# Two accumulating DMAs in another order on GpSimd's queue

## The reference, cut to what matters

```python
def swiglu_ffn(h, w_gu, w_down):
    g, u = jnp.split(h @ w_gu, 2, axis=-1)
    return (jax.nn.silu(g) * u) @ w_down       # mid: 512 x 2816, w_down: 2816 x 1024
...
x = x + 0.5 * swiglu_ffn(rmsnorm(x, n_ffn2[i]), ffn2_w_gu[i], ffn2_w_down[i])
```

## Time and profile before

| what | value |
|---|---|
| median of 3 runs | 1913.32 us (1913.1 to 1913.39) |
| the profiled execution | 1913.59 us |
| its span, first to last instruction | 1911.9 us |
| TensorE busy in it | 1901.3 us (99%) |
| VectorE, ScalarE, GpSimd busy | 1433.0, 1017.2, 361.8 us |
| mean granted TensorE clock | 0.999 of full speed |
| chain that ended last, by engine | PE 96%, DVE 2%, ACT 1%, issue 1% |

### The profile page before, as it was taken

The page is one execution under the profiler, slowest core; times in us unless marked ns, Lnnn a source line. Parts: engine busy times, 40 slices in busy tenths (PEclk is TensorE's granted clock), DMA queues, the critical chain, the costliest instruction groups (busy, mean ns, idle before and its releaser), DMA issues.

```text
span 1911.9 us, 33151 instructions
## 1 busy us (share of the span) xinstructions
PE 1901.3 (99%) x12350; PEld 1740.7 (91%) x12350; DVE 1433.0 (75%) x2272; ACT 1017.2 (53%) x1705; POOL 361.8 (19%) x357
## 2 busy tenths in 40 slices
PE   9999999999999999999999999999999999999998
PEld 7998998888898889999999999899898889999986
DVE  7865885687765658888888985687577658878887
ACT  7542654356554546555556653355356445555655
POOL 2200212100102212222021120121232113532020
PEclk9999999999999999999999999999999999999999
DMA  6744974323434625999598592596354336999695
GB/s 183 160 110 115 180 157 135 124 67 104 118 120 133 189 79 127 186 183 189 167 228 181 133 182 91 134 184 150 96 177 153 89 89 144 205 213 207 200 229 129
DMA packets 396623, 288.53 MB, mean 151 GB/s; under 512 B 19826, under 2 KB 362992, under 8 KB 396512
## 3 DMA queue, kind: packets, MB, share of 16 engines
q1 hardware_dynamic: 299456, 208.69, 36.8%
q0 software_dynamic: 88128, 76.36, 25.0%
q10 hardware_dynamic: 8928, 2.11, 0.5%
HBM read 276.63 MB, written 10.49 MB: 150 GB/s over the span
## 4 chain that ended last, share of the span: by engine, by line
PE 96%; DVE 2%; ACT 1%; issue 1%; DMA 0%; ACTq 0%; DVEq 0%
PE ps L489 15%; PE ps L491 15%; PE ps L490 15%; PE ps L1294 14%; PE ps L1293 14%; PE ps L1292 14%; PE ps L1161 3%; PE ps L1163 3%; PE ps L1162 3%; DVE w_lo L2458 1%; ACT w_hi L1677 0%; PE ps L1218 0%; PE ps L1141 0%; DVE sums L3426 0%; DVE x L2981 0%
## 5 line engine op out<-in xcount | busy, mean ns | idle before, releaser
L2458 DVE TENSOR_TENSOR w_lo<-raw,w_hi 128x512 fp32r<-128x512 f32 (+5 forms) x367 | 384.0, 1061 | 217.2 <-ACT w_hi L1677 216.7
L1677 ACT ACTIVATE w_hi<-raw 128x512 fp32r<-128x512 f32 (+5 forms) x367 | 331.7, 923 | 177.6 <-PE ps L491 124.0
L1292 PE MATMUL ps<-s_hi,w_hi 128*128 128x256 f32 x1248 | 353.2, 283 | 0.0
L1293 PE MATMUL ps<-s_lo,w_hi 128*128 128x256 f32 x1248 | 353.2, 283 | 0.0
L1294 PE MATMUL ps<-s_hi,w_lo 128*128 128x256 f32 x1248 | 353.2, 283 | 0.0
L1293 PE MATMUL ps<-h_lo,w_hi 128*128 128x256 f32 x936 | 264.9, 283 | 0.0
L1294 PE MATMUL ps<-h_hi,w_lo 128*128 128x256 f32 x936 | 264.9, 283 | 0.0
L1292 PE MATMUL ps<-h_hi,w_hi 128*128 128x256 f32 x936 | 264.9, 283 | 0.0
L1292 PEld LDWEIGHTS ps<-s_hi,w_hi 128*128 128x128 f32 x1248 | 239.6, 192 | 0.0
L1293 PEld LDWEIGHTS ps<-s_lo,w_hi 128*128 128x128 f32 x1248 | 239.6, 192 | 0.0
L1294 PEld LDWEIGHTS ps<-s_hi,w_lo 128*128 128x128 f32 x1248 | 239.6, 192 | 0.0
(11 more groups left out here) (465 smaller groups left out, 4317.0 us busy)
## 6 DMA issues: line engine op xcount, KB each, us to landing
raw<-in_ffn_w_gu SPq DMA_DIRECT2D x106, 512.0 KB, 5.0
outer_even<-in_ffn_w_gu SPq DMA_DIRECT2D x70, 256.0 KB, 3.6
outer_even<-in_ffn_w_gu POOLq DMA_DIRECT2D x70, 256.0 KB, 6.4
raw<-in_ffn_w_gu SPq DMA_DIRECT2D x68, 256.0 KB, 6.1
raw<-in_x_w_kv SPq DMA_DIRECT2D x16, 1024.0 KB, 5.8
outer_odd<-in_ffn_w_gu SPq DMA_DIRECT2D x62, 256.0 KB, 3.8
outer_odd<-in_ffn_w_gu POOLq DMA_DIRECT2D x62, 256.0 KB, 7.0
raw<-in_ffn_w_down SPq DMA_DIRECT2D x16, 768.0 KB, 4.4
```

Source lines behind the costliest of these rows:

```text
L1292: nc.tensor.matmul(to, hi[:, kk, :], right_hi, start=fresh, stop=False, skip_group_check=True)
L1293: nc.tensor.matmul(to, hi[:, kk, :], right_lo, start=False, stop=False, skip_group_check=True)
L1677: return nc.scalar.activation(out_ap, in_ap, ACT.Copy, **kw)
L2458: return nc.vector.tensor_tensor(out_ap, value, hi.bitcast(F32), ALU.subtract)
```

## The change

At the end of `add_down_sums`, `add_third(0)` now stands ahead of `add_fourth(1)`. GpSimd thus issues F0, T0, F1, T1, T2, F2 where it issued F0, F1, T0, T1, T2, F2. The waits of each piece and all other instructions are as they were. This holds for both seven-product runs.

```diff
                 add_fourth(0)
+                add_third(0)
                 add_fourth(1)
-                add_third(0)
                 add_third(1)
                 add_third(2)
                 add_fourth(2)
```

## The result

The changed kernel is slower: 1917.68 us (median of nine runs, 1916.26 to 1920.15) against 1913.37 us for the kernel before (nine runs, 1913.10 to 1914.19). That is 4.31 us, a ratio of 1.0022 with a 95% interval from 1.0013 to 1.0030. The forecast was 1915.6 us, and the time lies above its range, which ended at 1917.0 us. The profiled execution after took 1916.26 us with a span of 1914.5 us. It is the quickest of the nine, so its trace shows 2.7 us where the median shows 4.3 us, and a part of the loss has to be looked for in other executions.

A forecast was written before the change was run, and what follows sets the result against it. TensorE was taken as the bound, busy 1901.3 us of a 1911.9 us span. Block 1's 0 us plus the last run's 2.3 us on the 1913.32 us median gave 1915.6 us; range 1912.8 to 1917.0 us.

The forecast's parts named there:

- the hole after F0: Last run: DMA engines idle from about 1860.5 us until T0's data move, where they used to carry F1.
- the first stall: Last run: TensorE's 0.41 us stand ahead of k = 30, set by T0's landing, would go.
- a new wait of TensorE at k = 32: Last run: T1 lands 2.45 us late, so TensorE stands about 2.5 us there.
- the first two: Rivals: T1 lands where it did, 1913.3 us, 18%; pieces pass so quickly that both TensorE stalls go, about 1911.8 us, 7%.
- The third: Rival: F1 between T0 and T1 takes 7.7 us, T1 is late by 5.1 us; 1918.4 us, 8%.
- a cover of 1.2 us ... 0 us: Block 1: T1 lands 1.5 us late, but k = 32 is ready 1.2 us before TensorE starts it; cost 0 us.
- if TensorE waits in block 1: Block 1: the prediction named a TensorE wait there as showing it wrong, having expected none.
- I take 2.3 us for the last run: Last run: cost taken as 2.3 us, between VectorE's 2.45 us delay and TensorE's 2.0 us.
- 8.5 + 2 x 5.05: T0 lands 8.5 us after issue into an empty queue, then F1 and T1 follow at 5.05 us each.
- tied to TensorE rather than to VectorE: Last run: if ScalarE's start of k = 39 or 40 follows TensorE, the shift there is 2.0 us.
- some 13 us: Last run: T1 would land some 13 us after its own issue, at about 1879.5 us.
- the second stall: Last run: TensorE's 1.14 us stand ahead of k = 40 would keep some 1.6 us, ending at about 1901.4 us.

The follow-up runs named there:

- the half piece: Changed kernel with F1 cut in the last run into two DMAs of two rows, the first between T0 and T1, the second behind T2: 1914.76 us.
- the filled kernels: Changed kernel with twelve small matmuls into an unread PSUM bank ahead of k = 31 of the last run, run twice: 1918.19 us and 1918.70 us.

## Why the prediction was wrong

**Right, as the prediction put it:** the hole after F0 (the engines were empty from 1861 to 1862 us); T0 landing 8 to 9 us after its issue (9.0 us); F1 about 5 us behind it (5.05 us); the first stall gone; ScalarE idle for T1; a new wait of TensorE at k = 32 (3.16 us for some 2.5 us). T1's landing was put at 1879.5 us and came at 1879.74 us. Of the rivals, the first two are out: T1 did not land where it did, and nothing became faster. The third is out as a mechanism, since F1 took 4.6 to 5.9 us behind T0 in the five traces with this order in the last run, and not 7.7 us; that its 1918.4 us lies nearer to the measured 1917.68 us than the forecast does came about by other terms. The sign was right, and the order of the pieces on q0 was the cause, as the three places of F1 and the half piece show.

**The step that failed first: "a cover of 1.2 us ... 0 us" for block 1.** T1 was to be ready 1.5 us late there, 18.6 us after T0's issue. In the traces with this order ScalarE reads it 19.9 to 20.4 us after that issue, against 17.18 us before, so it is 2.8 to 3.2 us late. The cover before the change was 1.2 + 1.5 = 2.7 us. T0's own issue scatters too: counted from the ruler's first step it comes from 0.5 us earlier to 0.65 us later than before. Both together put T1's split 2.3 to 3.9 us later on the ruler. Less the cover of 2.7 us that is nothing in two of the seven traces and 0.5 to 1.2 us in five, and TensorE's waits at k = 32 are just that: none that the view of waits lists in two, 0.57 to 1.18 us in five. That block 1 also widens the spread of the times is not shown: it is 3.9 us over nine runs after and 1.1 us over nine before, but the kernel before has 2.8 to 4.2 us in the three later sets. The prediction's last test, "if TensorE waits in block 1", is the one that it fell by.

**The term that was mis-sized: "I take 2.3 us for the last run".** It is 3.5 us, and this is the larger miss. T1's distance grew from 16.17 to 19.61 us, where 8.5 + 2 x 5.05 = 18.6 us was reckoned. The distance is 19.59 to 19.67 us in all five traces with this order in the last run, though its parts change: T0 lands 8.4 to 10.0 us after its issue, F1 4.6 to 5.9 us behind T0, T1 5.1 to 5.5 us behind F1. With F1 behind all of the third sum, T0 and T1 alone take 14.25 to 14.49 us, where the prediction's prices give 8.5 + 5.05 = 13.55 us, and F1 between them adds some 5.3 us. So about 0.7 us of the missing 1.0 us is T0 and T1 themselves, and 0.3 us is F1. And the cut from 2.45 to 2.3 us for steps "tied to TensorE rather than to VectorE" was not due: the tail stays within 0.1 us of 34.8 us in all kernels in which T1 sets the pace, so T1's lateness goes to the end one for one. That T1's landing at 1879.74 us came so near to the forecast is partly luck, as T0 was issued 0.77 us earlier in this execution than in that of before.

**The sum:** 3.5 us in the last run and 0.7 us in block 1 make 4.2 us, against 4.31 us between the medians. That they agree so closely is partly luck, as the same kernel read +5.79 us elsewhere. In the one profiled execution it is 3.44 us for T1's distance, less 0.77 us for the earlier T0 and 0.07 us for the tail: 2.6 us, the difference of the spans. Two of the prediction's signs failed besides. T1 landed 15.0 us after its own issue and not some 13 us, as that issue came 1.43 us earlier than before. And the second stall, "still there" by the prediction, is gone: the slow clock took its time, at no cost.

**Open:** why T0 and T1 take 0.7 us more than their prices, and why the parts of the 19.6 us change from trace to trace. Why the changed kernel read +4.3 us once and +5.8 us, over five runs, the other time is not settled either: the intervals overlap, and in the profile of the second the span is 4.9 us longer than before, of which 3.5 us is T1's distance, 0.8 us block 1 and the remaining 0.6 us lies outside both. Executions of one kernel differ by as much: from the ruler's end to T0's issue the changed kernel takes 795.99 us in one trace and 797.11 us in the other.

## What to carry to other kernels

Here the pieces of one queue landed in the order of their issue, and 1024 KB put in between held up the next by some 5.3 us. Before one is moved, look at what will stand ahead of the next piece that someone waits for, and at which hole in the transfers the moved one had been filling. A cover of about a microsecond behind a DMA is to be counted as a part of its price, not as nothing, when the landing, or the issue behind it, can shift by half of that. And a single profiled execution can be the one in which a wait does not show; a ruler between two steps that all kernels share finds it in the others.

## What was not expected of the hardware

TensorE's granted clock fell to 0.50, the lower of its two levels (1.2 GHz), for about 3 us after it had stood for 3.16 us (the changed kernel), 3.84 us (the same, run again), 3.86 us (the new order in the last run alone) and 2.06 us (F1 ahead of T2). After the gaps of 1.14 us before and of 0.64 to 1.48 us in the filled kernels it stayed at 1.00. The Trainium skill, TensorE: Matmul & The Clock Gate, section Part 1: The HAM clock gate, has an idle array fall to 1.2 GHz and activity bring back 2.4 GHz; the traces here agree, with 0.50 after the long gaps and 1.00 again later, in the changed kernel's first profile by 1887 us. What this case adds is that such a fall can be free, where another engine sets the pace and TensorE would otherwise wait later (1918.95 us with it, 1918.70 us without).
